# Gate product signals its tiles, retention statistics one chunk later, output product in halves

## The reference, cut to what matters

```
x = x + rmsnorm(f, ffn_post_norm)
e = rmsnorm(p @ w_ple_proj, ple_norm)
x = x + sigmoid(x @ w_ple_gate) * e          # the gate
hn = rmsnorm(x, mix_norm_g)                  # second block
q, k, v, g = split(hn @ ret_w_in)            # 4 heads, q and k 256 wide, v and g 512 wide
q, k = rope(q), rope(k) / 16
o = decayed (q k^T) v, centred and normalised per head, times a gain
h = x + (silu(g) * o) @ ret_w_out
h = h + (relu(rmsnorm(h) @ mlp_w1) ** 2) @ mlp_w2
```

## Time and profile before

| What | us |
|---|---|
| median of three runs | 2041.4 |
| time of the profiled execution | 2041.12 |
| its span in the trace | 2038.9 |
| PE busy in the span | 1993.7 (98%) |
| DVE, POOL, ACT busy | 964.7, 951.3, 771.6 |
| mean granted TensorE clock | 0.997 of full |

### The profile page before, as it was taken

How to read it: one execution, slowest core, us unless ns; L and a number is a source line. 1 busy time by engine, 2 the same in 40 slices (tenths; PEclk the granted TensorE clock), 3 DMA queues, 4 the chain that set the end, 5 groups by cost and what they waited for, 6 DMA issues and landing times.

```text
span 2038.9 us, 24121 instructions
## 1 busy us (share of the span) xinstructions
PE 1993.7 (98%) x9364; PEld 1643.9 (81%) x9364; DVE 964.7 (47%) x1419; ACT 771.6 (38%) x1099; POOL 951.3 (47%) x682
## 2 busy tenths in 40 slices
PE   6999999999999999999999999999999999999998
PEld 5777778888887788888887888888888888888887
DVE  5558553332257754545455231325466674132234
ACT  6446442321244442424244231323355554232232
POOL 4423445455564535353535544545433335554552
PEclk9999999999999999999999999999999999999999
DMA  5312247376222313131312233233322223233231
GB/s 158 91 42 73 93 90 99 105 117 110 89 83 96 112 62 104 62 103 62 103 62 95 91 104 103 83 102 100 105 82 82 82 83 100 87 104 103 85 100 62
DMA packets 164544, 186.99 MB, mean 92 GB/s; under 512 B 4009, under 2 KB 150193, under 8 KB 164337
## 3 DMA queue, kind: packets, MB, share of 16 engines
q1 hardware_dynamic: 162784, 181.68, 27.8%
q10 hardware_dynamic: 1424, 3.67, 4.2%
q0 software_dynamic: 256, 0.55, 0.1%
HBM read 180.77 MB, written 4.72 MB: 91 GB/s over the span
## 4 chain that ended last, share of the span: by engine, by line
PE 72%; issue 11%; POOL 9%; DVE 4%; ACT 2%; DMA 0%; SPq 0%; POOLq 0%; DVEq 0%; ACTq 0%
PE ps L685 23%; PE ps L686 22%; PE ps L687 22%; POOL w_lo L632 9%; PE ps L837 2%; PE ps L849 1%; PE ps L858 1%; PE ps L859 1%; DVE hn_lo L1790 1%; DMA o_buf<-in_x 0%; ACT w_hi L1190 0%; DVE scr L1765 0%; PE ps L721 0%; DVE scr L2203 0%; DVE x L2177 0%
## 5 line engine op out<-in xcount | busy, mean ns | idle before, releaser
L632 POOL TENSOR_TENSOR w_lo<-raw,w_hi 128x512 fp32r<-128x512 f32 x652 | 926.9, 1452 | 1017.2 <-ACT w_hi L1190 1017.2
L685 PE MATMUL ps<-hn_hi,w_hi 128*128 128x512 f32 x1528 | 609.9, 399 | 14.4 <-DVE hn_lo L1790 8.2
L687 PE MATMUL ps<-hn_hi,w_lo 128*128 128x512 f32 x1528 | 597.2, 391 | 0.0
L686 PE MATMUL ps<-hn_lo,w_hi 128*128 128x512 f32 x1528 | 597.0, 391 | 0.0
L1190 ACT ACTIVATE w_hi<-raw 128x2048 fp32r<-128x2048 f32 x163 | 312.3, 1916 | 738.9 <-PE ps L687 731.8
L685 PEld LDWEIGHTS ps<-hn_hi,w_hi 128*128 128x128 f32 x1528 | 288.0, 188 | 86.9 <-issue 12.0
L685 PE MATMUL ps<-hid_hi,w_hi 128*128 128x512 f32 x888 | 348.4, 392 | 5.7 <-POOL w_lo L632 1.5
L686 PE MATMUL ps<-hid_lo,w_hi 128*128 128x512 f32 x896 | 348.9, 389 | 0.0
L687 PE MATMUL ps<-hid_hi,w_lo 128*128 128x512 f32 x888 | 345.7, 389 | 0.0
L686 PEld LDWEIGHTS ps<-hn_lo,w_hi 128*128 128x128 f32 x1528 | 288.1, 189 | 61.7 <-issue 4.3
L687 PEld LDWEIGHTS ps<-hn_hi,w_lo 128*128 128x128 f32 x1528 | 287.8, 188 | 60.8
(11 more groups left out here) (290 smaller groups left out, 1862.3 us busy)
## 6 DMA issues: line engine op xcount, KB each, us to landing
raw<-in_mlp_w SPq DMA_DIRECT2D x64, 1024.0 KB, 5.2
raw<-in_ret_w_in SPq DMA_DIRECT2D x24, 1024.0 KB, 5.1
raw<-in_att_w_in SPq DMA_DIRECT2D x12, 1024.0 KB, 5.2
raw<-in_w_gate SPq DMA_DIRECT2D x11, 1024.0 KB, 5.4
raw<-in_w_up SPq DMA_DIRECT2D x11, 1024.0 KB, 5.4
raw<-in_w_in SPq DMA_DIRECT2D x8, 1024.0 KB, 5.5
raw<-in_w_down SPq DMA_DIRECT2D x8, 1024.0 KB, 8.2
raw<-in_ret_w_out SPq DMA_DIRECT2D x8, 1024.0 KB, 5.1
```

Source lines behind the costliest of these rows:

```text
L632: ins = pool.tensor_tensor(w_lo[:, slot, at], raw[:, slot, at], w_hi[:, slot, at].bitcast(F32), ALU.subtract)
L685: pe.matmul(o, hi, rhs_hi, start=start, stop=False, skip_group_check=True)
L686: pe.matmul(o, hi, rhs_lo, start=False, stop=False, skip_group_check=True)
L687: return pe.matmul(o, lo, rhs_hi, start=False, stop=stop, skip_group_check=True)
```

## The change

- GATE chunk 2 is used in tile order 0 to 7 and starts on pieces of its low part (`parts_ready`; POOL signals `w_part` for it). GATE chunk 3 goes in tile order, and after tile k is read for both m, PE raises `gate_read`. ACT writes the next `hn_hi` tiles 0 to 5 behind these signals, before the last gate group is complete. ACT's split of GATE 2 stands one copy later.
- DVE's low parts and sums are reordered; most sums come last. ACT's squares too, with the splits of RET 1 and RET 2 between them. The statistics on PE move from between RET 0 and RET 1 to the seventh tile of RET 1. In the first head ACT's split of RET 3 still stands ahead of k's high parts.
- The output product's first two groups are done by halves: tiles 0, 1 for both groups, then tiles 2, 3 for both. The split of RET 6 comes before a table load.
- In the last head DVE's low parts of a group's two x tiles come after the next group's adds.

The waits on tiles and POOL's loop are unchanged otherwise (POOL does the same chunks in the same order, in two loops with four chunks written out between them).

```diff
...
+            def parts_ready(c, earlier):
+
+                def wait(k):
+                    if k == 6:
+                        chunk_ready(c)
+                    elif k % 2 == 0:
+                        pe.wait_ge(s["w_part"], earlier + k // 2 + 1)
+                return wait
+
+            product(WOUT.chunk(2), WOUT.group(2), KD, 256, 0, hn_hi, hn_lo, parts_ready(WOUT.chunk(2), 0))
...
-            for m in range(2, 4):
-                chunk_ready(GATE.chunk(m))
-                gate_product(m, GATE_ORDER, None)
+            gate_product(2, range(KD), parts_ready(GATE.chunk(2), 3))
+            chunk_ready(GATE.chunk(3))
+            for k in range(KD):
+                ins = gate_product(3, [k], None, k == 0, k == KD - 1)
+                if k < 6:
+                    ins.then_inc(s["gate_read"], 1)
 
...
+            def both_stats(k):
+
+                if k == 6:
+                    stat_columns(N_RET)
+                    stat(N_RET)
+
             def head(h, first=False):
                 for n in range(2):
                     chunk_ready(RET.chunk(n, h))
                     product(RET.chunk(n, h), RET.group(n, h), KD, 256, 0, hn_hi, hn_lo,
-                            normed(N_RET) if first and n == 0 else None)
-                    if first and n == 0:
-                        stat_columns(N_RET)
-                        stat(N_RET)
+                            (normed(N_RET), both_stats)[n] if first else None)
                 values_half(h, 0)
 
...
-                for n in range(4):
-                    c = RET.chunk(6 + n // 2, h)
-                    if n % 2 == 0:
-                        chunk_ready(c)
-                    product(c, RET.group(6 + n, h), 4, 512, 2 * (n % 2), hid_hi[:, 12:16, :],
+                def out_half(n, half):
+
+                    product(RET.chunk(6 + n // 2, h), RET.group(6 + n, h), 4, 512, 2 * (n % 2), hid_hi[:, 12:16, :],
                             hid_lo[:, 12:16, :],
-                            (lambda k: pe.wait_ge(s["ret_y_lo"], h * 4 + k + 1)) if n == 0 else None)
+                            (lambda k: pe.wait_ge(s["ret_y_lo"], h * 4 + k + 1)) if n == 0 else None,
+                            range(2 * half, 2 * half + 2), half == 0, half == 1)
+
+                chunk_ready(RET.chunk(6, h))
+                for n, half in ((0, 0), (1, 0), (0, 1), (1, 1)):
+                    out_half(n, half)
+                chunk_ready(RET.chunk(7, h))
+                for n in (2, 3):
+                    out_half(n, 0)
+                    out_half(n, 1)
 
...
                 act.wait_ge(s["ple_x"], 2 * n + 2)
                 act.activation(hn_hi[:, t, :], x[:, t, :], ACT.Copy).then_inc(s["ple_xhi"], 1)
-                if n == GATE_SPLIT + 1:
+                if n == GATE_SPLIT + 2:
                     group_ready(GATE.group(0))
                     split(GATE.chunk(2))
-                if n == GATE_SPLIT + 2:
+                if n == GATE_SPLIT + 3:
                     for m in range(2):
                         copy_out(GATE.group(0), m, aux[:, m, :])
...
                 if m < 3:
                     split(GATE.chunk(m + 2))
-                if m == 3:
-                    for t in range(2):
-                        gained_hi(N_RET, t, ("mix_norm_g_2", t))
                 for t in range(2):
                     act.wait_ge(s["ple_e"], 2 * (2 * m + t) - 3)
                     copy_out(g, t, aux[:, 2 + t, :], ACT.Sigmoid)
-                if m == 3:
-                    for t in range(2, 6):
-                        gained_hi(N_RET, t, ("mix_norm_g_2", t))
-                    split(GATE.chunk(5))
                 if m == 1:
-                    for t in range(2):
+                    for t in range(4):
                         act.wait_ge(s["ple_e"], 2 * (t + 1))
                         square(N_RET, t, x[:, t, :])
-                for t in range(2):
-                    act.wait_ge(s["ple_e"], 2 * (2 * m + t + 1))
-                    if m == 3:
-                        gained_hi(N_RET, 6 + t, ("mix_norm_g_2", 6 + t))
-                    square(N_RET, 2 * m + t, x[:, 2 * m + t, :])
+                if m == 2:
+                    for t in range(6):
+                        act.wait_ge(s["gate_read"], t + 1)
+                        act.wait_ge(s["ple_e"], 2 * (t + 1))
+                        gained_hi(N_RET, t, ("mix_norm_g_2", t))
+            split(RET.chunk(1))
+            for t in (6, 7):
+                act.wait_ge(s["ple_e"], 2 * (t + 1))
+                gained_hi(N_RET, t, ("mix_norm_g_2", t))
+            square(N_RET, 4, x[:, 4, :])
+            group_ready(RET.group(0))
+            split(RET.chunk(2))
+            for t in range(5, KD):
+                square(N_RET, t, x[:, t, :])
 
             act.dma_start(aux[:, :, :], T["c_decay"]).then_inc(s["decay_in"], 16)
...
-                    split(RET.chunk(n + 2, h))
+                    if n or not first:
+                        split(RET.chunk(n + 2, h))
...
                 act.activation(rstd[:, :], rstd[:, :], ACT.Exp, scale=-0.5).then_inc(s["ret_rstd"], 1)
+                group_ready(RET.group(4, h))
+                split(RET.chunk(6, h))
                 act.preload_act_table_set("silu_and_others")
                 for n in range(2):
                     g = RET.group(4 + n, h)
                     group_ready(g)
-                    if n == 0:
...
-            for m in range(3):
+            for m in range(2):
                 for t in range(2):
                     gated(m, t)
-                    if 2 * m + t >= 2:
-                        sums(N_RET, 2 * m + t - 1)
-
-            for t in range(2):
+            sums(N_RET, 1)
+            sums(N_RET, 2)
+            gated(2, 0)
+            gained_lo(N_RET, 0, ("mix_norm_g_2", 0))
+            gated(2, 1)
+            for t in range(1, 4):
                 gained_lo(N_RET, t, ("mix_norm_g_2", t))
             gated(3, 0)
-            sums(N_RET, 5)
-            gained_lo(N_RET, 2, ("mix_norm_g_2", 2))
+            gained_lo(N_RET, 4, ("mix_norm_g_2", 4))
             gated(3, 1)
-            for t in range(3, 7):
+            for t in range(5, KD):
                 gained_lo(N_RET, t, ("mix_norm_g_2", t))
-            sums(N_RET, 6)
-            gained_lo(N_RET, 7, ("mix_norm_g_2", 7))
-            sums(N_RET, 7)
+            for t in range(3, KD):
+                sums(N_RET, t)
 
 
...
                         add_to(g, m, x[:, 2 * n + m, :])
-                    if last_head:
-                        for t in (2 * n, 2 * n + 1):
+                    if last_head and n:
+                        for t in (2 * n - 2, 2 * n - 1):
                             gained_lo(N_MLPA, t, ("mlp_norm_g_2", t))
 
             with dve.Fori(0, RH - 1) as h:
                 head(h)
             head(RH - 1, last_head=True)
+            for t in (6, 7):
+                gained_lo(N_MLPA, t, ("mlp_norm_g_2", t))
             all_sums(N_MLPA)
 
             def mlp(ph, norm, base, next_norm, next_gain):
...
```

More of the change, by code:

```diff
@@ L207 @@
  two_s two_mx two_nmx two_exp two_rs two_p two_t two_hi two_lo two_pv two_shift two_o two_ohi two_olo
- gate_old_hi gate_old_lo gate_old_done gate_e_hi gate_e_lo gate_e_done gate_scaled gate_sum gate_sig
+ gate_old_hi gate_old_lo gate_old_done gate_e_hi gate_e_lo gate_e_done gate_scaled gate_sum gate_sig gate_read
  mlp_sq mlp_hi mlp_lo att_in_hi att_in_lo tab_scaled ffn_silu ffn_part fin_tmp fin_t fin_left fin_right""".split()
@@ L669, in _ @@
             first = WOUT.chunk0 + 4
-            loops = (N_CHUNKS - first) // 2
-            with pool.Fori(0, loops) as i:
+            before = (GATE.chunk0 + 2 - first) // 2
+            with pool.Fori(0, before) as i:
                 lo(first + 2 * i, first % 2)
                 lo(first + 1 + 2 * i, (first + 1) % 2)
-            for c in range(first + 2 * loops, N_CHUNKS):
+            for c in range(first + 2 * before, GATE.chunk0 + 4):
+                lo(c, c % 2, parts=c == GATE.chunk0 + 2)
+            first = GATE.chunk0 + 4
+            after = (N_CHUNKS - first) // 2
+            with pool.Fori(0, after) as i:
+                lo(first + 2 * i, first % 2)
+                lo(first + 1 + 2 * i, (first + 1) % 2)
+            for c in range(first + 2 * after, N_CHUNKS):
                 lo(c, c % 2)
@@ L1613, in head @@
                     group_ready(g)
-                    if n == 0:
-                        split(RET.chunk(6, h))
                     for m in range(2):
```

## The result

| | before | changed |
|---|---|---|
| median, us | 2041.47 | 2045.64 |
| range over 20 runs each, us | 2040.81 to 2042.68 | 2040.64 to 2047.18 |
| profiled execution, its span | 2041.12, 2038.9 | 2041.43, 2039.3 |

The ratio changed to before is 1.0015, interval 1.0009 to 1.0021. The median is 2.8 above the upper end of the forecast range, and the time went up where 2.2 less was forecast. The runs of before lie within 1.9 us. The changed kernel's fall in two groups: five between 2040.6 and 2043.0 at a mean granted clock of 0.997 to 0.998, and fifteen between 2044.1 and 2047.2 at 0.994 to 0.996. The profiled execution is one of the five; for none of the fifteen is there a trace. So there are two questions: why the change wins nothing at full clock, and what costs 4 us in the other fifteen.

A forecast was written before the change was run, and what follows sets the result against it. PE, busy for 98% of the span, was taken as the bound. The terms -1.5 (RET 0), +2.8 (scores), -3.7 (output), -1.4 (last head) and +1.6 (clock) sum to -2.2: 2039.2 us as median, range 2035.8 to 2042.8.

The forecast's parts named there:

- Output product, -3.7: Output product, four heads: waits for the third low tile (2.05) and RET 6's low weights (1.67) go, gain 3.7.
- The bounds 2.0 to 3.7: Output product's gain: 2.0 if only the third tile's wait goes, up to 3.7.
- The rival with no gain: Output product gains nothing because PE waits for the first low tile instead of the third: 2042.9; chance 0.05.
- Late statistics, +2.8: At the scores: later 1/rms delays q's and k's rotation, a new PE wait of 2.8; bounds 0 to 7.6.
- S + 18.1: When scores can start, S being the start of the statistics; PE has work until S + 15.4.
- Clock, +1.6: One of two new waits, at RET 0's sixth tile and the scores, brings 1.2 GHz: 1.6; bounds 0 and 3.2.
- The rival "both": Waits at RET 0's sixth tile and the scores both bring the lower clock: 1.6 more, 2040.8; chance 0.22.
- my reason against the first: The wait in RET 0 is soon cut up by other small waits, which hide part of the slower pace.
- RET 0, -1.5: Gate to RET 0's end: 1.77 before its second tile goes, 3.0 comes at its sixth; gain 1.5.
- Gate, 0: GATE 2 and 3: shorter gate tile wait, but GATE 3's low weights limit it; 0, bounds gain 0.9, loss 0.2.
- Last head, -1.4: Last head: PE's wait for a bank goes with the addition ahead of low parts; gain 1.4, bounds 1.0 to 1.5.
- Statistics themselves: no wait: RET 1's seventh tile: last sum ready 7.8 after RET 0's end, PE there 8.2 after; no wait, 0.4 to spare.

The follow-up runs named there:

- e2: The kernel before with only the output product by halves, RET 6's earlier split and the last head's order; 2041.04 us, ratio 0.9995.
- e9: e2 with ACT's split of RET 7 moved ahead of the logarithm's table load; 2035.76 us, ratio 0.9968.
- e6: The kernel before with only the statistics at RET 1's seventh tile and the split of RET 2 ahead of 1/rms; 2047.04 us, ratio 1.0023.
- e11: The changed kernel with the last squares ahead of the wait for RET 0's group and statistics at RET 1's third tile; 2039.3 us, ratio 0.9985.
- e10: The changed kernel with the split of RET 7 ahead of the logarithm's table load; 2040.5 us, ratio 0.9988.
- e1: The changed kernel run again without any edit; 2044.44 us, ratio 1.0012 to the kernel before.
- e3: The kernel before with only the gate signals, order of the next normed tiles and statistics at RET 1's seventh tile; 2047.09 us, ratio 1.0024.
- e7: The changed kernel with 10 useless matmuls ahead of RET 0's tile 5 alone; 2043.85 us, ratio 1.0009.
- e4: The changed kernel with useless matmuls, 10 ahead of RET 0's tile 5 and 12 ahead of the first v matmul; 2042.38 us, ratio 1.0001.
- e5: The changed kernel with the split of RET 7 ahead of the second group's silus, before the table load; 2052.59 us, ratio 1.0052.
- e8: e2 with the split of RET 7 ahead of the second group's silus, before the table load; 2047.91 us, ratio 1.003.

## Why the prediction was wrong, by its own steps

- **Output product, -3.7: this step failed.** The waits it counts did go, in all four heads. But PE came 0.94 earlier to RET 7, and I followed the gain to the next wait only for the first low tile, not for the next low weights. Before, they were ready 0.1 ahead of PE's first use of them (POOL and then PE in the trace of before):

```profile
763.75 5.05 POOL L632 TENSOR_TENSOR w_lo<-raw,w_hi 128x512 fp32r<-128x512 f32 x4 [6.68 <-ACT w_hi L1190]
```

```profile
768.91 0.44 PE L685 MATMUL ps<-hid_hi,w_hi 128*128 128x512 f32 x1
```

After, POOL starts them at 764.22 and ends at 769.25, and PE, which could start at 768.2, starts at 769.30. The bounds 2.0 to 3.7 assumed nothing late behind the product. Measured from one head to the next, after: 767.96 to 869.80, 971.74 and 1073.67 are 101.84 to 101.94 per head, and before 861.77 to 963.72 and 1065.63 are 101.95 and 101.91. The gain is 0, where 3.7 was said (for all four heads together the starts give a loss of 0.12). The rival with no gain named the right size, and the wrong place (the first tile). e2 shows it with the part alone, e9 that RET 7's weights are the cause.
- **Late statistics, +2.8: size nearly right, place wrong.** The wait is 2.98 and stands at the first v matmul, one chunk before the scores. The prediction counted k's chain to the scores and passed over who else waits for the rotation: the pair of banks. The wait at v then hid the one at the scores: k's low parts end at 710.81, the last v matmul starts at 710.88. The chain to the scores was itself forecast well (S + 18.1, measured S + 18.4); that the chain over the banks ends within 0.3 of it, so that the size came out (the stretch grew by 3.28), is luck. Shown by e6, and by e11, where it goes.
- **Clock, +1.6: too small, and one value for a thing that varies.** Both waits can bring 1.2 GHz (e10 has both falls, e1 and e3 the first alone, e7 the second alone behind a filled first). They cost about 1.3 net for the first and 1.3 to 2.9 for the second. By their times, in fifteen of the first twenty executions at least one fell; which, no trace shows. The rival "both" was the right mechanism, with 1.6 for the second where e10 shows up to 2.9; my reason against the first (cut up by small waits) does not hold, e1 shows its 0.66. The Trainium skill, "TensorE: Matmul & The Clock Gate", section "Why this matters for your kernels", warns of just this, and the runs agree with it in direction: with the idle time filled (e4) the clock is 1.00 in every window from 670 to 710 us. But the fall is not certain: the 3.37 at 263.52 in the first trace was followed by full clock.
- **RET 0, -1.5: nearly right.** Measured -1.33. The wait for tile 5 is 2.63 where 3.0 was said, but one for the low part of tile 1 (0.25 by the row, 0.41 by the starts) was not in the sum. Ahead of the first matmul there is none, as said.
- **Gate, 0:** measured -0.80, inside its bounds; GATE 3's low weights end at 658.49 (POOL 651.76 and 6.73), which is 659.15 on the clock of before, where the execution is 0.66 later, against 659.26; ACT's split is not late.
- **Last head, -1.4: right.** Before, 1.46 were lost by starts; after, that wait is gone (e2, too).
- **Statistics themselves: no wait, right.** The sums end at 691.8, PE is there at 692.44.

Corrected sum at full clock: -0.80 - 1.33 + 3.28 + 0.12 (heads) - 1.46 (last head) = -0.2, a kernel equal to before; with -0.66 from the start of the kernel and +1.3 from its end that is 0.4 over before, as the profiled spans are (2039.3 and 2038.9). The other 4.2 up to the median of 2045.64 is put down to the clock: by the traces 2.6 (e5) to 4.1 (e10) where both waits bring it, and up to 2 in the feed-forward start. How it divides in the fifteen is not shown, for want of a trace.

What stays open: why a wait of the same length brings the lower clock in one execution and not in another (2.65 in e1 and 2.63 in the first trace), and why the slow stretch behind the v wait has twice the length in e7 and e10 that it has in e5 and e6. No run here sets that. Whether any of the end's 1.3 is the change was not tried either.

## What to carry to other kernels

Follow a gain until it has passed every later supply of the engine: a wait of 0.1 to spare behind it takes it all back, and the engine that supplies (here ACT's order, a table load ahead of a split) has to be moved with it. When a result is moved later, list everything that its readers hold, PSUM banks first, and not only the data. Here many small waits that together cost as much as one long one were the better kind, since the long one could cost its clock as well.

## What the runs showed of the hardware

- Idle times of 2.6 and 3.0 us on PE are followed by 1.2 GHz in some executions of the same kernel and not in others. The slow stretch has about 8 starts behind the first wait; behind the second it has 6 to 8 in e5 and e6 and 14 in e7 and e10. Waits of 2.0 us were followed by it as well: one of four in e8 (0.66 in the window from 870 us) and two of four in e5. Between 600 and 1140 us none of the waits of 1.8 us or less was.
- DVE steps on two SBUF operands take 1.5 to 1.7 beside POOL's subtractions and 0.65 apart from them. In e8 a POOL chunk that starts 4.6 us earlier than in e2 (760.43 instead of 765.07) falls on four such steps and costs 3.9 us of DVE time (3.07 + 3.45 instead of 1.29 + 1.30).
- A table load of 1.28 us on ACT, moved behind one split, is worth 4.9 us over the four heads.
